# A hybrid decoder step on one Trainium2 core: the FFN's gate and up projections as 2x2 blocks with seven block products for eight, and the down projection moved behind them through DRAM

## The reference

```python
def swiglu(x, w_gate, w_up, w_down):
    return (jax.nn.silu(x @ w_gate) * (x @ w_up)) @ w_down

h = h + rmsnorm(y, norm_g[i, 1])
h = h + rmsnorm(swiglu(rmsnorm(h, norm_g[i, 2]), w_gate[i], w_up[i], w_down[i]), norm_g[i, 3])
h = h + jax.nn.sigmoid(h @ w_ple_gate[i]) * (p[i] @ w_ple[i])
```

## Time and profile before

| | |
|---|---|
| median of 3 runs | 3127.33 us (3124.76 to 3129.07) |
| profiled execution, first to last instruction | 3127.3 us |
| mean granted TensorE clock | 0.996 |
| TensorE busy (matmuls) | 3075.6 us, 20352 matmuls |
| VectorE, ScalarE, GpSimd busy | 1567.8, 903.5, 262.2 us |
| transfers | 247.46 MB, 79 GB/s |

### The profile page before, as it was taken

The page is one execution under the profiler, slowest core; times in us unless marked ns, Lnnn a source line. Parts: engine busy times, 40 slices in busy tenths (PEclk is TensorE's granted clock), DMA queues, the critical chain, the costliest instruction groups (busy, mean ns, idle before and its releaser), DMA issues.

```text
span 3127.3 us, 51548 instructions
## 1 busy us (share of the span) xinstructions
PE 3075.6 (98%) x20352; PEld 2942.6 (94%) x20352; DVE 1567.8 (50%) x2613; ACT 903.5 (29%) x1600; POOL 262.2 (8%) x317
## 2 busy tenths in 40 slices
PE   8999999999999999999999999999999999999999
PEld 8999999999999999999977886569999999999998
DVE  5444284444444447453335665553744444444472
ACT  4111351111111116332235553343411111111262
POOL 1000010000000001000015551110100000000011
PEclk9999999999999999999999999999999999999999
DMA  3111111111111121113257865961111111111112
GB/s 107 45 44 47 42 39 43 48 41 48 46 42 48 41 62 41 41 48 112 98 154 160 162 119 222 395 249 40 42 44 46 48 41 48 41 48 47 57 48 71
DMA packets 229210, 247.46 MB, mean 79 GB/s; under 512 B 19061, under 2 KB 183925, under 8 KB 228994
## 3 DMA queue, kind: packets, MB, share of 16 engines
q1 hardware_dynamic: 204978, 164.65, 17.7%
q0 software_dynamic: 24016, 79.77, 8.3%
HBM read 209.50 MB, written 18.10 MB: 73 GB/s over the span
## 4 chain that ended last, share of the span: by engine, by line
PE 82%; DVE 4%; issue 2%; ACT 1%; DMA 1%; POOL 0%; SPq 0%; DVEq 0%; ACTq 0%; POOLq 0%
PE psum L2273 20%; PE psum L2275 20%; PE psum L2274 20%; PE psum L2857 2%; PE psum L2299 2%; PE psum L2843 2%; PE psum L2293 2%; PE psum L2294 2%; PE psum L2828 1%; PE psum L2829 1%; PE psum L2796 1%; PE psum L2797 1%; PE psum L2798 1%; PE psum L2922 1%; PE psum L2976 1%
## 5 line engine op out<-in xcount | busy, mean ns | idle before, releaser
L2273 PE MATMUL psum<-xs_hi,w_hi 128*128 128x384 f32 (+1 forms) x2592 | 848.9, 327 | 2.6 <-DVE w_lo L1478 2.4
L2275 PE MATMUL psum<-xs_hi,w_lo 128*128 128x384 f32 (+1 forms) x2592 | 845.5, 326 | 0.0
L2274 PE MATMUL psum<-xs_lo,w_hi 128*128 128x384 f32 (+1 forms) x2592 | 844.9, 326 | 0.0
L2273 PEld LDWEIGHTS psum<-xs_hi,w_hi 128*128 128x128 f32 x2592 | 486.6, 188 | 3.7 <-DVE w_lo L1478 3.7
L2274 PEld LDWEIGHTS psum<-xs_lo,w_hi 128*128 128x128 f32 x2592 | 486.7, 188 | 0.0
L2275 PEld LDWEIGHTS psum<-xs_hi,w_lo 128*128 128x128 f32 x2592 | 486.5, 188 | 0.0
L865 ACT ACTIVATE w_hi<-raw 128x1024 fp32r<-128x1024 f32 x192 | 202.4, 1054 | 618.9 <-DVEq L1501 596.9
L1859 DVE TENSOR_TENSOR y<-y,psum 128x384 f32<-128x384 f32 x528 | 268.8, 530 | 155.2 <-PE psum L2275 155.2
L2275 PE MATMUL psum<-hid_hi,w_lo 128*128 128x384 f32 (+1 forms) x1056 | 346.0, 328 | 0.0
L2273 PE MATMUL psum<-hid_hi,w_hi 128*128 128x384 f32 (+1 forms) x1056 | 345.6, 327 | 0.0
L2274 PE MATMUL psum<-hid_lo,w_hi 128*128 128x384 f32 (+1 forms) x1056 | 345.1, 327 | 0.0
(11 more groups left out here) (326 smaller groups left out, 4322.2 us busy)
## 6 DMA issues: line engine op xcount, KB each, us to landing
kpage<-in_cache_k SPq DMA_DIRECT2D x64, 512.0 KB, 8.5
v_page<-in_cache_v POOLq DMA_DIRECT2D x64, 512.0 KB, 5.8
raw<-in_w_gate SPq DMA_DIRECT2D x44, 512.0 KB, 3.7
raw<-in_w_up SPq DMA_DIRECT2D x44, 512.0 KB, 3.7
raw<-in_w_down SPq DMA_DIRECT2D x44, 512.0 KB, 3.8
raw<-in_w_in SPq DMA_DIRECT2D x24, 512.0 KB, 3.6
raw<-in_w_v SPq DMA_DIRECT2D x24, 512.0 KB, 3.4
raw<-in_w_ple_gate SPq DMA_DIRECT2D x16, 512.0 KB, 3.5
```

Of the source, the lines that this page charges most:

```text
L2273: M(out, wh, xh, start=first, stop=False)
L2274: M(out, wh, xl, start=False, stop=False)
L2275: return M(out, wl, xh, start=False, stop=last)
```

## The change

- **Which groups.** Group 1 stays (`first_pair` and two `block8`). Gate and up of groups 2 to 11 become 20 units a layer, gate and up in turn. A unit is one projection of a group: 256 columns, 1024 channels, 1088 tokens. Its weight is cut in 2x2 blocks of 512 channels by 128 columns, the input in 2x2 blocks of 512 channels by 544 tokens.
- **Products.** A unit is seven products of a sum of weight blocks with a sum of input blocks, each with 4 chunks and two sides of 272 tokens, three matmuls each (`product`). They go in the order R11, F2, R12, F3, F1, R22, F4 through three pairs of PSUM banks.
- **Sums of the input** (once a layer): GpSimd multiplies `h` by the gains (`gained`, 12 instructions of 544 elements, `tensor_scalar`), and adds and subtracts blocks (5 `tensor_tensor` of 2176 elements); ScalarE and VectorE split the sums into high and low (`t_high`, `t_low`), `t4` in place of a block of `xs_hi` and `xs_lo`.
- **Sums of the weights** (each unit): SP loads two slabs (`pair`), GpSimd makes four sums in five `tensor_tensor` of 512 elements (`third_form`, `second_form`, `first_form`, `fourth_form`); ScalarE and VectorE split all seven forms (`form_high`, `form_low`); the high parts go through a ring of three.
- **Results.** VectorE adds the products up from PSUM (`part`, seven additions of 544 a unit, one copy by ScalarE). Of a gate, GpSimd multiplies by `rbB` twice (`normed`, `gate_ready`: 8 `tensor_tensor` of 544 a group), ScalarE takes the sigmoid, VectorE multiplies (`gate_act`); of an up unit VectorE multiplies with the gate (`hidden`).
- **Through DRAM.** SP stores the product of gate and up (`store`, four a group). The down products of all 11 groups come after the last unit: SP loads `hid_raw` (1.1 MB a group, three buffers), ScalarE and VectorE split it (`hidden_high`, `hidden_low`), and `down` goes on as before, with a copy in place of the first addition, so that `y` is no longer set to zero.
- The loops of SP, ScalarE and VectorE in the FFN are written out. Semaphores are shared to make room for the new ones (`page_landed`, `state_stored`); `conv` and attention keep their work.

The core of the diff (GpSimd's `ffn`, VectorE's `gate_unit` and its callers, TensorE's `product` and its callers):

```diff
-STAGES = [("in", 24, 24), ("out", 8, 8), ("ffn0", 66, 132), ("pp0", 2, 8), ("pg0", 8, 8),
+STAGES = [("in", 24, 24), ("out", 8, 8), ("ffn0", 4, 4), ("skip0", 4, 0), ("dn0", 22, 88), ("pp0", 2, 8),
...
             def ffn(layer):
...
                 pool.wait_ge(h_dve, 6 * layer + 6)
-                pool.memset(y[:, :, :], 0.0).then_inc(y_zero, 1)
+                gained(t3_high, 0, slice(HALF, T))
+                gained(t3_low, 4, slice(HALF, T))
+                pool.wait_ge(t_sum, 8 * layer + 2)
+                G_TT(t3_low[:, :, :], t3_low[:, :, :], t3_high[:, :, :], ALU.subtract).then_inc(t_sum, 1)
+                gained(t1_high, 0, slice(0, HALF))
+                third_form(U0)
+                second_form(U0)
+                first_form(U0)
+                pool.wait_ge(t_sum, 8 * layer + 4)
+                pool.wait_ge(tok_std, TOKS * layer + 2 * NT)
+                G_TT(t2_low[:, :, :], t3_low[:, :, :], t1_high[:, :, :], ALU.add).then_inc(t_sum, 1)
+                G_TT(t1_low[:, :, :], t3_high[:, :, :], t1_high[:, :, :], ALU.subtract).then_inc(t_sum, 1)
+                pool.wait_ge(t_hi, 4 * layer + 2)
+                G_TT(t3_lo[:, :, :], t3_low[:, :, :], t3_hi[:, :, :].bitcast(F32), ALU.subtract).then_inc(t_sum, 1)
+                fourth_form(U0)
+                pool.wait_ge(t_lo, 4 * layer + 2)
+                G_TT(t4_low, t4_low, t2_lo[:, :, :].bitcast(F32), ALU.subtract).then_inc(t_sum, 1)
+                for U in range(U0, U0 + UNITS):
+                    more = U + 1 < U0 + UNITS
+                    if more:
+                        third_form(U + 1)
+                        second_form(U + 1)
+                    if U % 2 == 0:
+                        normed(U, 0)
+                    if more:
+                        first_form(U + 1)
+                    if U % 2 == 0:
+                        normed(U, 1)
+                        gate_ready(U, 0)
+                        normed(U, 2)
+                    if more:
+                        fourth_form(U + 1)
+                    if U % 2 == 0:
+                        normed(U, 3)
+                        for q in range(1, 4):
+                            gate_ready(U, q)
...
+                def gate_unit(U):
...
+                    form_low(U, F3)
+                    second_parts(U)
+                    if first:
+                        t_low(t1_lo[:, :, :], t1_low[:, :, :], t1_hi[:, :, :], 3)
+                    form_low(U, F1)
+                    gate_part(U, 0, R12, s1)
+                    form_low(U, R22)
+                    third_parts(U)
+                    if first:
+                        t_low(t4_lo, t4_low, t4_hi, 4)
+                    form_low(U, F4)
...
+                    gate_part(U, 1, F1, s3)
+                    part(U, F1, s2, s2)
+                    gate_act(G, 0)
+                    form_low(U + 1, R11)
+                    gate_part(U, 2, R22, s3)
+                    form_low(U + 1, F2)
...
+                    gate_part(U, 3, F4, s2)
+                    gate_act(G, 1)
+                    form_low(U + 1, R12)
...
+                for U in range(U0, U0 + UNITS, 2):
+                    gate_unit(U)
+                    up_unit(U + 1)
...
+                lo(dn0)
+                hidden_low(0)
+                for g in range(GROUPS - 1):
+                    down(g)
...
+                def product(U, j, *waits):
...
+                    pe.wait_ge(form_lo, k + 1)
...
+                    xh, xl = MOVING[j]
+                    for side in range(2):
+                        n = slice(QUAD * side, QUAD * side + QUAD)
+                        for c in range(4):
+                            wc = slice(c * P, (c + 1) * P)
+                            ins = three(psum[:, 2 * bank_of(U, j) + side, 0:QUAD], high[k % RING][:, wc], low[U % 2][j][:, wc],
+                                        xh[:, c, n], xl[:, c, n], c == 0, c == 3)
+                    ins.then_inc(product_done, 1)
...
-                gate_up(n0, b0, True)
-                for g in range(10):
-                    gate_up(n0 + 6 * g + 4, b0 + 12 * g + 4)
-                    down(n0 + 6 * g + 8, b0 + 12 * g + 8, c0 + 2 * g + 2, g % 2)
-                down(n0 + 64, b0 + 124, c0 + 22, 0, True)
...
+                for U in range(U0, U0 + UNITS):
+                    unit(U)
+                for g in range(GROUPS):
+                    down(g)
```

More of the change, by code:

```diff
@@ L82 @@
 A_MISC = A_RB + 4352
+GROUPS = D_FF // (2 * P)
+UNITS = 2 * (GROUPS - 1)
+HALF = T // 2
+QUAD = HALF // 2
+R11, F2, R12, F3, F1, R22, F4 = range(7)
+PRODUCTS = 7
+FORMS = 5
+PARTS = 7
+TAKEN = (2, 4, 6, 7)
+RING = 3
+HIDS = 3
+QUARTERS = ((0, 0), (1, 1), (1, 0), (0, 1))
 def trunk(nc, ins, outs):
@@ new lines, in trunk, with raw_of, hi_of, lo_of @@
+    BUFS = [form_buffers(layer) for layer in range(2)]
+    FIRST_DOWN = (SLAB0["dn0"], SLAB0["dn1"])
+    down_raw = sb("down_raw", [P, 1024], F32, A_STG)
+    down_lo = sb("down_lo", [P, 1024], F32R, A_STG)
+    down_hi = sb("down_hi", [P, 1024], F32R, A_STG + 4096)
+    def raw_of(n):
+        return down_raw if n in FIRST_DOWN else raw[n % RAWS]
+    def hi_of(n):
+        return down_hi if n in FIRST_DOWN else w_hi[n % HLS]
+    def lo_of(n):
+        return down_lo if n in FIRST_DOWN else w_lo[n % RAWS]
@@ L533, in ffn, with gate_up @@
[L533 to L540, removed]
+                n0, b0, dn0 = SLAB0[name], BLK0[name], SLAB0[f"dn{layer}"]
+                def gate_up(u):
+                    load(n0 + u, cols((wg, wu)[u % 2], (u // 2) * P), C, P)
@@ new lines, in form_high @@
+                def form_high(U, j):
+                    k = PRODUCTS * U + j
+                    if j in (R11, R12, R22):
+                        act_e.wait_ge(pair_landed[U % 2], 32 * (U // 2 + 1) + KEY_PAGES * layer)
+                    else:
+                        act_e.wait_ge(forms_made, FORMS * U + {F3: 1, F2: 2, F1: 4, F4: 5}[j])
+                    if U == U0 and j < RING:
+                        act_e.wait_ge(acc_ready, NT * (b0 + 3))
+                    else:
+                        act_e.wait_ge(product_done, k - RING + 1)
+                    A(high[k % RING][:, :], form[U % 2][j][:, :], ACT.Copy).then_inc(form_hi, 1)
@@ new lines, in form_low, with t_low @@
+                def form_low(U, j):
+                    k = PRODUCTS * U + j
+                    dve.wait_ge(form_hi, k + 1)
+                    dve.wait_ge(forms_made, FORMS * U + {R11: 3, F2: 3, R12: 4, F3: 2, F1: 3, R22: 2, F4: 5}[j])
+                    TT(low[U % 2][j][:, :], form[U % 2][j][:, :], high[k % RING][:, :].bitcast(F32), ALU.subtract)\
+                        .then_inc(form_lo, 1)
+                def t_low(dst, src, hi_part, k):
+                    dve.wait_ge(t_hi, 4 * layer + k)
+                    TT(dst, src, hi_part.bitcast(F32), ALU.subtract).then_inc(t_lo, 1)
@@ new lines, in t4_first, with part @@
+                def t4_first():
+                    dve.wait_ge(acc_ready, NT * (b0 + 4))
+                    dve.wait_ge(t_hi, 4 * layer + 1)
+                    for c in range(4):
+                        ins = V.scalar_tensor_tensor(t4_low[:, c, :], h[:, 4 + c, 0:HALF], vecT[:, 4 + c, row:row + 1],
+                                                     t2_hi[:, c, :].bitcast(F32), ALU.mult, ALU.subtract)
+                    ins.then_inc(t_lo, 1)
+                def part(U, j, out, other):
+                    dve.wait_ge(product_done, PRODUCTS * U + j + 1)
+                    TT(wide(out), product_of(U, j), wide(other), ALU.add).then_inc(part_taken, 1)
@@ L2618, in p_turned, with down @@
                     ins.then_inc(p_tr, 1)
-                def down(n, blk, chunks, par, last=False):
-                    pe.wait_ge(hid_ready, chunks * NT + NT)
+                def down(g):
+                    n, blk, r, last = dn0 + 2 * g, dblk + C * g, g % HIDS, g == GROUPS - 1
+                    pe.wait_ge(hid_ready, GROUPS * layer + g + 1)
                     for s in range(2):
```

585 lines of the change are left out of this document (432 added, 153 removed).

## The result

The changed kernel takes 3190.73 us (median of 4 runs, 3186.22 to 3194.52) against 3127.93 of before in the same series: a ratio of 1.0202, interval 1.0188 to 1.0217. It is 2% slower. The forecast was 3118, the range ended at 3147. The profiled execution has a span of 3192.9 us, 65.6 more than before.

The account below looks back on a forecast made before the run. The FFN was taken as bound by TensorE's matmul count times their distance. Per layer 48.2 - 36.6 - 6.8 = 4.8 us gained, 9.6 for two: 3127.3 - 9.6 = 3117.7, rounded 3118, range 3070 to 3147.

Parts of the forecast that it names:

- End of the units: Between last unit and down products: TensorE idle 5.3 us plus 1.5 for clock, 6.8 us a layer; later down phase unchanged.
- The 0.3 us: Down phase: VectorE needs 5.6 us after a slab's last tile to its next release; six tiles last 5.9, so no wait.
- Gain of fewer columns: Gate and up matmuls: 336 of 272 columns replace 288 a group, gaining 4.8 us a group, 48.2 us a layer.
- Steady units at 0: Middle gate and up units: VectorE and GpSimd contested work 38.0 of 42.6 us, tightest chain holds by 1.3; cost 0.
- The rival in which the exclusion reaches them: Steady units: the 1.3 us in hand to R12 is lost; groups at 44.0 us give 3145, slower; chance 25%.
- The exclusion: VectorE instructions with two SBUF inputs and GpSimd ones reading SBUF exclude each other for a whole instruction; PSUM-input ones unaffected.
- The rival without exclusion: FFN start: TensorE waits some 12 us a layer, set by GpSimd's own chain, giving 3070 us; chance 15%.
- the first step of the start: FFN start: VectorE's 8 `low` alternate with GpSimd's 8 `gained`, ending at 9.0 us; third slab's `lo` 7.9 late.
- Start of each FFN, 36.6 us: FFN start: TensorE waits of 34.3 us plus about 2.3 for the clock, 36.6 us a layer, uncertain by 8.
- the 2.3 us: FFN start: clock cost a layer; half-clock stretches worth 1.7 us each after long waits, mostly running into the next wait.
- the 0.9 chosen: FFN start: GpSimd's 544-column multiplication by a gain assumed 0.9 us, the middle between 0.46 and 1.4.
- The sum without the down phase: Whole layer: 48.2 gained less 36.6 at the start and 6.8 at the units' end, 4.8 us a layer gained.

Follow-up runs that it names:

- experiment 6: Against experiment 1: GpSimd makes the first subtraction of `fourth_form` twice in all 40 units; 3113.14 us, measured once.
- experiment 4: Kernel before plus unneeded GpSimd work: 100 two-input additions in layer 0's FFN, 100 memsets in layer 1's; 3130.34 us, measured once.
- experiment 5: Against experiment 1: the twelve multiplications by the gain at each FFN's start move from GpSimd to ScalarE; 3093.00 us, ratio 0.9902 to before.
- Experiment 8: Against experiment 7: the five 2176-column additions and subtractions at each FFN's start move from GpSimd to VectorE; 3067.76 us, ratio 0.9822 to before.
- experiment 1: Changed kernel, SyncE's down-phase load of group g+3's hidden values replaced by group g+2's, so no whole-group wait precedes slab loads; 3098.17 us, ratio 0.9907 to before.
- experiment 2: Against experiment 1: the wait for the end of group g put back ahead of the slab loads, the 1.1 MB transfer still behind them; 3124.98 us, measured once.
- experiment 3: Against experiment 1: VectorE's `lo` and `hidden_low` for the first down group go ahead of the last product's sums; 3099.42 us, ratio 0.9906 to before.
- experiment 7: Against experiment 5: VectorE's first down slab and hidden-value splits placed ahead of the last unit's third part for R22; 3090.39 us, ratio 0.9888 to before.

## Why the prediction was wrong

**The step that failed** is in "End of the units": "The rest of the down phase keeps its matmuls [...] no wait, by 0.3." It cost 45 and 46 us in the two layers, 91 in all. The sum there took each slab as landed in time and looked only at VectorE's order. In the kernel before, the gate and up products of a group, 47 us, lay between two groups of down products. With all down products in a row, a group is 23.7 us of matmuls, and SyncE spends the whole of it in one wait, with the next slabs behind it. The working followed each slab from its landing on and never asked what stands ahead of its issue in SyncE's queue. The 0.3 us is also where the warning was: a chain of 5.6 us in 5.9 leaves no room for a slab that is late by 3.5. The range was too narrow for the same reason: no case in it had a wait in most down groups (8 of 11).

**Gain of fewer columns:** right, and a little low. 288 x 0.165 = 47.5 us before (4424 matmuls in 730 us). After, the gate units of two middle groups start 42.2 us apart, 0.1256 us for each of 336 matmuls: 5.3 us a group for 4.8 forecast.

**Steady units at 0:** right, in both FFNs. The rival in which the exclusion reaches them is refuted, and experiment 6 shows that it was near: one more GpSimd instruction begins to cost.

**The exclusion:** right for GpSimd's instructions with two inputs, by experiment 4 and by the changed kernel itself. VectorE's groups there, shapes apart (busy us, mean ns of one):

```profile
L2181 DVE TENSOR_TENSOR form_low<-pair,form_high 128x512 fp32r<-128x512 f32 x160 | 194.1, 1222 | 43.5 <-POOL form L876 36.5 <-ACT form_high L1386 5.5 <-issue 1.4
L2211 DVE TENSOR_TENSOR gbuf<-gbuf,sig_part 128x544 f32<-128x544 f32 x80 | 102.9, 1286 | 0.0
L2201 DVE TENSOR_TENSOR second_part<-psum,first_part 128x544 f32<-128x544 f32 x40 | 28.7, 717 | 22.6 <-PE psum L2749 22.6
L2187 DVE TENSOR_TENSOR t_lo<-t_low,t_hi 128x2176 fp32r<-128x2176 f32 x4 | 17.8, 4442 | 0.0
```

With both inputs in SBUF they are nearly twice their length alone (0.68, 0.71, 2.42); with one in PSUM they keep it. The rival without exclusion is refuted.

It was wrong for `gained`, GpSimd's multiplication by the gains, and so the first step of the start failed too. The prediction let VectorE's eight `low` take turns with eight `gained` and end at 9.0 us in place of 4.0. They met from the start and took 4.54:

```profile
427.95 4.54 DVE L2060 SCALAR_TENSOR_TENSOR xs_lo<-h,vecT,xs_hi 128x320 fp32r<-128x320 f32 x8
428.23 7.64 POOL L841 TENSOR_SCALAR t_high<-h,vecT 128x544 f32<-128x544 f32 x4 [21.68 <-DVE h L2050]
```

Four or five of VectorE's instructions ran within one `gained` of 2.2 us, and one of them was longer, 0.92 us for 0.54. No run shows why this instruction differs. The Trainium skill ("Who interferes with whom", SBUF — State Buffer) has an exclusive lock between VectorE with two inputs in SBUF and a GpSimd instruction that reads SBUF, not with one that only writes it. The trace agrees for GpSimd's additions and for the memset; for `gained`, which reads SBUF, it shows no wait for the whole instruction.

**Start of each FFN, 36.6 us:** the sum was about right by luck, since its parts were not. In layer 0 TensorE is 0.8 us late at the third slab, where 7.9 were forecast. GpSimd's first wide subtraction holds up not that slab's `lo` but `hsq`, and TensorE waits 5.27 us for `hs`, a wait that the prediction didn't have. Then it waits 4.94 for R11, 5.67 for F2, 4.74 for F1 and 2.71 for R22, where 8.1, 7.2 + 0.4, 5.6 and 5.1 were forecast. That is 24.1 us for 34.3. But the clock cost far more than the 2.3 us. From 436.07 to 925.17 us are 489.1; 3360 matmuls at 0.1256, 144 at 0.165 and 36 small ones at 0.11 are 449.7; less the wait at the end, 34.3 are lost at the start, so 11.0 us are not waits. The granted clock shows them (window of layer 0's start):

```profile
454.00:520.00 66.00, 47.56 (x277) 46.66 (x278) 55.28 (x51) 20.10 (x27) 46.65 (x20) 0.82 0.10 34
```

The granted clock is at 1.2 GHz in five stretches, each of which begins near the end of one of the five waits, 23.9 us together; TensorE is busy for 19.6 of them, and half of that is 9.8. The 1.7 us for each that was scaled from the earlier trace rows was taken to be mostly hidden in the next wait; it was not. `gained` took 1.64 us with VectorE idle and 1.84 in the median of 16, far above the 0.9 chosen and above the upper bound of 1.4; in experiment 5, without it on GpSimd, the FFNs are 4.1 and 6.4 us shorter. Experiment 8 shows that the rest of the start's cost is for a good part the wide additions.

**End of the units, 6.8 us:** right. 5.12 us of waiting, at 5.3 forecast, and a clock of 0.83 from 925 to 935 us in experiment 1, which is 1.7 us.

**The sum without the down phase:** 4.8 us a layer forecast, 12.5 and 11.0 in experiment 1. The differences are 7.7 and 6.2. Columns are 5.0 of each, the start some 1.5 and 0.3, and a wait of 1.2 us that before had for `w_lo` in its FFN is gone. That leaves less than 0.5 us.

**The attention** has the same instructions in all versions, and its length between the marks is 974.5 before, 972.5 after, 967.1 in experiment 1, and 973.6, 975.4, 973.8, 973.1, 977.1 and 973.9 in experiments 2, 3, 5, 6, 7 and 8. So experiment 1 has 7.4 us over before that are not the change's. In the trace before, TensorE waits 3.9 us there for the `w_lo` of the earlier trace rows and 4.3 us at L2828, where no releaser is shown. In experiment 1 the first is 0.8 us, since the two instructions of the earlier trace rows don't meet, and the second is gone. The clock has no part in it: its stretches at 1.2 GHz in this piece are 17.1 us before and 20.5 in experiment 1. Such gains are luck and hang on when other engines' instructions start; why the second wait is gone is open.

## What to carry to other kernels

When a phase is packed densely, write down for each load which waits stand ahead of it in its queue, and put a load that waits for a buffer behind all loads that don't need to; the order of one queue was worth 3% here. An engine that reaches for late data in its program order also holds what it should release, so the profile names the release and not the load: follow the wait back to the queue. A long instruction on an engine that excludes another costs its length on that other engine, and may be cheaper when the other makes it itself; and a wait moved is not a wait removed unless it lands in a gap.

## What the runs showed of the hardware

- GpSimd's multiplication of 544 columns by a value per partition took 1637 ns with VectorE idle and up to 2787 ns beside it, longer than its addition of two inputs of 544 at its shortest (1338 ns) and more than twice ScalarE's 740 ns. One input instead of two saved GpSimd nothing.
- The same multiplication did not hold up VectorE for its whole length: eight instructions with two inputs in SBUF took 4.54 us beside it for 4.01 alone, while a subtraction with two inputs of 2176 columns made an instruction of 0.8 us last 5.46.
- VectorE's `form_low` waited for whole wide instructions of GpSimd (4.82 us at 479.10 in experiment 5), and in the changed kernel `t_lo` of 2176 columns took 6.5 us against one GpSimd addition of 5.3.
- Waits of 3.3 to 4.6 us, one in each of eight down groups, went with a granted clock of 0.94 over the phase; a group took 29.4 us, where 144 matmuls at 0.165 are 23.8, so it lost some 5.6 us by a wait of 3.5. In experiment 2, with waits near 1.0 us in the same places, the clock was 1.00:

```profile
950.00:1190.00 240.00, 232.05 (x1396) 229.91 (x1395) 156.31 (x262) 46.70 (x38) 9.98 (x11) 1.00 0.25 87
```
